# Expert weights in a decoder step: gate and up loads cut into halves of four row blocks

## The chip, the cores and the metric

The kernel runs on one core of a Trainium2 chip, in one launch. The metric is the device time of that core in microseconds (us). One core has a matrix engine (TensorE, PE in the rows, its weight loads PEld), a vector engine (VectorE, DVE), a scalar engine (ScalarE, ACT), GpSimd (POOL) and SyncE (SP), which here issues nearly all of the DMA transfers. The engines run their own instruction streams and meet only at semaphores. Transfers run on 16 DMA engines that all queues share.

## The reference

One step of a two-layer decoder trunk for 256 prompt tokens and 64 sample tokens (320 in all), `D_MODEL` 1024. Layer 0 mixes with mLSTM heads and a short gated convolution, layer 1 with differential attention. Both then do memory attention and a mixture of experts. The change is in the mixture of experts, of which each layer has 32, with 256 hidden columns each, and all of whose weights are read:

```python
y = jnp.zeros_like(x)
for g in range(N_GROUPS):                       # 4 groups of 8 experts
    h = jax.nn.silu(jnp.einsum('nd,edf->nef', x, w_gate[g])) * jnp.einsum('nd,edf->nef', x, w_up[g])
    y = y + jnp.einsum('nef,efd->nd', h * gate[:, g, :, None].astype(h.dtype), w_down[g])
```

Each token uses two experts (top one group, top two in it). Gate, up and down weights are float32: 1 MB for each of the three matrices of an expert, 96 MB for a layer.

## The kernel before

The stages run one after the other: mLSTM, memory attention, experts of layer 0 (`moe`), then attention, memory attention, experts of layer 1, and the final norm. Only the two expert stages matter here.

**Work of an expert stage.** The tokens are gathered into slots by expert, and the experts are taken in `NPAIR` = 16 pairs. In the path that these inputs take, `rounds` is 1 and there is one step q for a pair. TensorE's order is written out by hand in `moe_pe`. A step has `up(q)` (L2369: for each of the 8 row blocks k, and each expert j of the pair, a matmul against gate and up columns, 512 wide), `weigh(q)` (L2382), `select(q)` (L2391), `combine` of an earlier step (L2413), `down` in two halves (L2444) and `transpose_h` (L2453). Up to q = 12 (`TURN`) the order is `up(q)`, `weigh(q)`, `select(q)`, `combine(q-2)`, `down(q-1)`; at 12 a `combine` and a second `down` follow, so that from q = 13 each step does its own `down(q)`.

**Buffers.** `gu` holds two pairs of gate and up weights (slot g % 2, 4 MB each, g counting pairs over both layers). `dws` holds two pairs of down weights (2 MB each), one in `arena` and one in `stg`.

**Loads.** SyncE issues them in program order, and a wait holds all that stand behind it. `load_up(l, p)` waits on `gu_used` until the pair two before has been used. For a step q > 0 that semaphore is raised in `weigh(q)`, after all of `up(q)`. Then it issues four transfers of 1 MB (L469). Only for the last pair of a layer it issues eight of 512 KB, whose second half raises `gu_tail`. `load_down(l, p)` (L478) waits on `dw_used`, which VectorE raises when it has taken the results of the down product two before, and issues two of 1 MB. The order is up(0), up(1), down(0), down(1), up(2), then up(p+1), down(p) for p from 2 to 11, and down(p), up(p+1) for p from 12. Behind the last of layer 0 stand four transfers of attention weights (L446). On TensorE the matmuls at k = 0 wait for `gu_in` of the slot:

```python
if q % rounds == 0 and k == 0:
    pe.wait_ge(gu_in[g % 2], 64 * (g // 2 + 1))
if q % rounds == 0 and k == 4 and p == NPAIR - 1:
    pe.wait_ge(gu_tail, 64 * (l + 1))
```

A row block is one of 8 successive rows that a partition holds (`(p k) f -> p k f`). So a partition's share of one matrix is 8 KB in a row, and half of it 4 KB in a row.

Of the kernel before, what the change touches and what calls it, by code (L numbers as in the profile page):

```python
# [27 lines left out]
NPAIR = NE // 2  # L28
# [104 lines left out]
def build(nc, a, o):  # L133
# [13 lines left out]
    def sem(name):  # L147
        return ctx.enter_context(nc.semaphore(name))
# [119 lines left out]
    def state(h):  # L268
# [76 lines left out]

    names = """const_in tab_in vec_in small_in x_in gate_in cst_ready vec_ps vec_ev tr_ps tr_ev w_hi w_lo w_used
        w_ev in_hi in_lo sq_ready sum_ready std_ready xn_ready gate_ps gneg_ready gln_ready rows_ready
# [4 lines left out]
        gsel_ready rexp_ready gate_ready rank_ps off_ready rc_in moe_done out_mem out_c out_direct ml_ps  # L352
        ml_ev cleared xt_ps xt_hi xt_lo pt_ev pk_ready gate_lo xg_ps xg_act xg_dve z_ps
        zs_act zs_dve zt_ps row_pad qd_ready kt_act kt_dve bs_ps bo_ps bo_ev qp_ready padded id_in mem_hi hsum_ev""".split()
    S = {n: sem(n) for n in names}
# [4 lines left out]
    gu_in = [sem("gu_in0"), sem("gu_in1")]  # L360
    gu_tail = sem("gu_tail")
    dw_in = [sem("dw_in0"), sem("dw_in1")]
# [74 lines left out]
    def _(sp):  # L437
# [73 lines left out]
        for name, n in STREAM:  # L511
# [398 lines left out]
    def mlstm_pool(pool, link):  # L910
# [8 lines left out]
        nc.gpsimd.memset(dmat[rows, :, 384:448], 0.0)  # L919
        nc.gpsimd.memset(wlast[rows, :, 0:8], 0.0).then_inc(S["row_pad"], 1)  # L920
        pool.wait_ge(S["rows_ready"], 1)
# [15 lines left out]
        pool.wait_ge(S["ei_ready"], HA)  # L937
        pool.wait_ge(S["row_pad"], 1)
        decay(0)
        pool.wait_ge(S["w_ev"], sum(UNIT["in_b"]))  # L940
        pool.wait_ge(S["decay_ready"], 1)
        nc.gpsimd.memset(vw[rows], 0.0).then_inc(S["row_pad"], 1)
        pool.wait_ge(S["row_pad"], 2)
        pool.wait_ge(S["ml_ev"], 1)
# [27 lines left out]
    def mlstm_pe(pe):  # L972
# [86 lines left out]
        def numerators(h):  # L1059

            filled = 2 * h - 1
            pe.wait_ge(S["ct_ev"], h + 1)
            if h:
                pe.wait_ge(S["h_ready"], h)
            else:
                pe.wait_ge(S["q_ready"], 1)
                pe.wait_ge(S["s_ready"], HA)
                pe.wait_ge(S["row_pad"], 1)
            for bank, left in ((6, None), (7, ones)):
                first = True  # L1070
                for (tile, n, c, w) in DGROUPS:
                    t0 = T - 64 if tile == 2 else 128 * tile
                    lhs = vtok[:, tile, 128 * h:128 * h + 128] if left is None else ones[:]
                    nc.tensor.matmul(ps[:, bank, t0:t0 + w], lhs, dmat[:, h, c:c + w], start=first, stop=False,
                                     skip_group_check=True)
                    first = False
                if left is None:
                    for b in range(NB):
                        last = nc.tensor.matmul(ps[:, bank, NP + NI * b:NP + NI * b + NI], c0T[:, b, :],
                                                qi[:, h, NI * b:NI * b + NI], start=False, stop=(b == NB - 1),  # L1080
                                                skip_group_check=True)
                        if h:
                            fill(filled, 1, (b,))
                else:
                    last = nc.tensor.matmul(ps[:, bank, NP:T], ones[:], qn[:, h], start=False, stop=True,
                                            skip_group_check=True)
            last.then_inc(S["num_ps"], 1)

        def updates(h):
            pe.wait_ge(S["vw_ready"], h + 1)  # L1090
            if h == 0:
                pe.wait_ge(S["w_ev"], UK)
                pe.wait_ge(S["row_pad"], 2)
            fill_ready(2 * h)
# [852 lines left out]
    def qkv_act(act):  # L1947
        for i in range(12):
            act.wait_ge(S["w_used"], QKV + i + 1)
            if i == 2:  # L1950
                act.wait_ge(S["padded"], 1)
            for g in TURNS.get(i, ()):
# [13 lines left out]
        act.wait_ge(S["padded"], 3)  # L1966
        act.wait_ge(S["rot_done"], 12)
# [29 lines left out]
    def qkv_dve(dve, link):  # L1997
# [51 lines left out]
        dve.wait_ge(S["rot_done"], 16)  # L2049
        dve.wait_ge(S["padded"], 3)  # L2050
        for m in range(2):
# [128 lines left out]
    def route_dve(dve, link, l):  # L2180
# [78 lines left out]
        def slots(c):  # L2259
            for i in range(3):  # L2260
# [19 lines left out]
        V.tensor_tensor(xnh[64:128, 2, KD, 0:NE], gate[64:128, 2], xnh[64:128, 2, KD, 0:NE], ALU.subtract  # L2280
                        ).then_inc(S["gate_lo"], 1)
        for r in range(1, ROUNDS):
# [7 lines left out]
    def moe_pe(pe, l, rounds):  # L2290
        M = ML[l]
        last_step = NPAIR * rounds - 1
        def gather_first():
            pe.wait_ge(S["cleared"], 3 * l + 3)
            pe.wait_ge(S["pk_ready"], 3 * l + 1)
            pe.wait_ge(S["xt_hi"], 6 * l + 6)
# [30 lines left out]
        def gather_next():  # L2327
            pe.wait_ge(S["pk_ready"], 3 * l + 2)
            for k in range(KD + 1):
# [25 lines left out]
        def up(q):  # L2355
# [17 lines left out]

# [482 lines left out]
    def _(pool):  # L2856
# [7 lines left out]
        for name in ("norm_mix_g", "norm_mem_g", "norm_ffn_g"):  # L2864
# [221 lines left out]
```

## Time and profile before

| | |
|---|---|
| median of 3 runs | 1285.54 us (1282.66 to 1286.66) |
| the profiled execution: time, span | 1284.15 us, 1282.8 us |
| TensorE busy | 1204.0 us, 94% of the span |
| VectorE, ScalarE, GpSimd busy | 46%, 31%, 11% |
| DMA: bytes, mean rate, packets | 340.52 MB, 265 GB/s, 114028 |
| mean granted TensorE clock | 0.983 of full speed |

The span is that of one profiled execution on the core; its own time is 1.35 us longer. The expert stage of layer 0 lies between 427 and 668 us of the span, that of layer 1 between 1028 and 1271 us. Times in the rows are counted from the span's start. A 1024.0 KB transfer is 1.049 million bytes, which is how GB/s is counted. "Busy" of a TensorE group counts overlapping matmuls once.

### The profile page before, as it was taken

To read this page: it belongs to the slowest core of one execution; us is meant where nothing else is said; L and a number is where in the kernel's file an instruction comes from. 1 tells how busy PE (TensorE), PEld (TensorE's weight loads), DVE (VectorE), ACT (ScalarE), POOL (GpSimd) and SP (SyncE) were. 2 spreads that over 40 slices of the span, in tenths; PEclk is the share of its full clock that TensorE was granted. 3 is DMA by queue.
4 is the path that set the end of the run, shared out by engine and by line. 5 is a ranking of instruction groups with operands and counts; after the bars stand their busy time and mean duration, and the time that the engine had idled before them with its cause. 6 is when DMAs were issued, how large, how long until landed. Compare 5 with 4: busy or idle time off the path is not lost.

```text
span 1282.8 us, 20881 instructions
## 1 busy us (share of the span) xinstructions
PE 1204.0 (94%) x8548; PEld 738.2 (58%) x8548; DVE 583.9 (46%) x1163; ACT 397.9 (31%) x739; POOL 146.7 (11%) x184
## 2 busy tenths in 40 slices
PE   6999999999998899999999998989999799999996
PEld 5866679877776433333336776767777544333332
DVE  3764368774545522211236667546455541222122
ACT  3533323263443111111125334454444211111113
POOL 5220022111001011000002230001000101001000
PEclk9999999899999899999999999999999899999999
DMA  9575354368659389999974477703775748999994
GB/s 302 155 227 151 102 172 141 115 221 316 228 185 397 134 334 420 420 421 423 419 279 132 135 250 259 256 8 100 296 304 199 321 197 334 416 421 420 421 418 168
DMA packets 114028, 340.52 MB, mean 265 GB/s; under 512 B 7598, under 2 KB 75514, under 8 KB 86272
## 3 DMA queue, kind: packets, MB, share of 16 engines
q1 hardware_dynamic: 108752, 323.51, 67.1%
q0 software_dynamic: 4736, 14.42, 3.6%
q8 instruction: 71, 1.16, 0.4%
q10 hardware_dynamic: 432, 1.11, 0.3%
q14 instruction: 37, 0.30, 0.1%
HBM read 328.48 MB, written 10.54 MB: 264 GB/s over the span
## 4 chain that ended last, share of the span: by engine, by line
PE 76%; DMA 8%; DVE 7%; ACT 5%; issue 2%; POOL 1%; SPq 0%; ACTq 0%; DVEq 0%; POOLq 0%
PE ps L2369 15%; PE ps L614 9%; PE ps L615 8%; PE ps L616 8%; PE ps L2444 6%; DMA arena<-in_w_exp_up 6%; PE ps L2413 4%; PE ps L1530 3%; DVE wl L608 2%; PE ps L1544 2%; PE ps L1569 2%; PE ps L1615 2%; PE ps L1633 2%; DMA stg<-in_w_mem_o 1%; ACT wh L600 1%
## 5 line engine op out<-in xcount | busy, mean ns | idle before, releaser
L2369 PE MATMUL ps<-arena,mkv 128*64 128x512 f32 x1024 | 226.4, 594 | 9.0 <-DMA arena<-in_w_exp_up 8.5
L614 PE MATMUL ps<-bx,wh 128*128 128x320 f16 (+2 forms) x688 | 192.4, 287 | 10.7 <-DVE wl L608 4.1
L615 PE MATMUL ps<-bx,wh 128*128 128x320 f16 (+2 forms) x688 | 192.6, 287 | 0.0
L616 PE MATMUL ps<-bx,wl 128*128 128x320 f16 (+2 forms) x688 | 192.3, 287 | 0.0
L608 DVE SCALAR_TENSOR_TENSOR wl<-stg,wh 128x1024 f16<-128x1024 f32 x122 | 154.6, 1307 | 50.1 <-ACT wh L600 50.1
L600 ACT ACTIVATE wh<-stg 128x1024 f16<-128x1024 f32 x122 | 122.5, 1050 | 146.2 <-PE ps L616 127.8
L2369 PEld LDWEIGHTS ps<-arena,mkv 128*64 128x64 f32 x1024 | 75.6, 137 | 153.9 <-issue 152.2
L2584 DVE TENSOR_TENSOR arena<-ps,arena 128x512 f16<-128x512 f32 x64 | 44.1, 689 | 160.6 <-ACT arena L2530 113.5
L2588 DVE COPY arena<-ps 128x1 f32<-128x1 f32 x32 | 5.1, 159 | 185.3 <-PE ps L2391 185.3
L614 PEld LDWEIGHTS ps<-bx,wh 128*128 128x128 f16 x688 | 68.7, 101 | 34.9 <-issue 14.7
L614 PE MATMUL ps<-arena,wh 128*128 128x320 f16 x288 | 86.6, 301 | 0.9 <-ACT mkv L1212 0.9
L2530 ACT CAST arena<-ps 128x512 f16<-128x512 f32 x64 | 37.5, 585 | 161.1 <-PE ps L2444 161.1
L2635 POOL COPY mkv<-bx 128x576 f32 x60 | 39.9, 668 | 415.1 <-PE ps L2391 301.2
L615 PE MATMUL ps<-arena,wh 128*128 128x320 f16 x288 | 86.5, 300 | 0.0
L616 PE MATMUL ps<-arena,wl 128*128 128x320 f16 x288 | 86.4, 300 | 0.0
L615 PEld LDWEIGHTS ps<-bx,wh 128*128 128x128 f16 x688 | 67.1, 98 | 20.4 <-issue 1.5
L616 PEld LDWEIGHTS ps<-bx,wl 128*128 128x128 f16 x688 | 67.3, 98 | 20.2
L2526 ACT ACTIVATE mkv<-ps 128x256 f32<-128x256 f32 x32 | 12.3, 384 | 214.2 <-PE ps L2369 214.2
L2413 PE MATMUL ps<-arena,rstd 128*128 128x512 f16 x360 | 74.0, 384 | 2.8 <-DVE arena L2584 2.8
L2444 PE MATMUL ps<-stg,mkv 128*64 128x512 f32 x256 | 60.4, 598 | 1.8 <-ACT mkv L2534 1.8
L2444 PE MATMUL ps<-arena,mkv 128*64 128x512 f32 x256 | 60.4, 598 | 0.9 <-ACT mkv L2534 0.9
L1530 PE MATMUL ps<-cst,arena 128*128 128x128 f32 x384 | 52.7, 280 | 3.6 <-ACT arena L1507 2.0
(438 smaller groups left out, 1782.3 us busy)
## 6 DMA issues: line engine op xcount, KB each, us to landing
arena<-in_w_exp_gate SPq DMA_DIRECT2D x60, 1024.0 KB, 12.1
arena<-in_w_exp_up SPq DMA_DIRECT2D x60, 1024.0 KB, 14.2
arena<-in_w_exp_down SPq DMA_DIRECT2D x32, 1024.0 KB, 15.0
stg<-in_w_exp_down SPq DMA_DIRECT2D x32, 1024.0 KB, 16.3
arena<-in_cache_mem_k SPq DMA_DIRECT2D x16, 1024.0 KB, 8.0
arena<-in_cache_mem_v SPq DMA_DIRECT2D x16, 1024.0 KB, 5.0
stg<-in_w_in_a SPq DMA_DIRECT2D x28, 512.0 KB, 4.7
stg<-in_w_qkv_c SPq DMA_DIRECT2D x20, 512.0 KB, 3.6
```

What stands on the lines that cost most here:

```text
L600: nc.scalar.mul(wh[:, s, c], src[:, c], WSCALE).then_inc(S["w_hi"], 1)
L608: nc.vector.scalar_tensor_tensor(wl[:, s, c], src[:, c], WSCALE, wh[:, s, c], ALU.mult, ALU.subtract).then_inc(S["w_lo"], 1)
L614: nc.tensor.matmul(out, wh[:, s, at:at + 128], hi, start=start, stop=False, **flags)
L615: nc.tensor.matmul(out, wh[:, s, at:at + 128], lo, start=False, stop=False, **flags)
L616: return nc.tensor.matmul(out, wl[:, s, at:at + 128], hi, start=False, stop=stop, **flags)
L1530: last = nc.tensor.transpose(ps[:, turn_bank(c, b, f), 256 * i + 128 * t:256 * i + 128 * t + 128], kpg[:, b % 2, t, at:at + 128], ident)
L2369: last = nc.tensor.matmul(ps[64 * j:64 * j + 64, UB, :], xe[:, q % 2, j, k, :], gu[:, g % 2, j, :, k, :], start=(k == 0), stop=(k == KD - ...
L2413: nc.tensor.matmul(out, csel[:, q % 3, 128 * i:128 * i + n], y[:, 512 * half:512 * half + 512], start=(first and y is yh), stop=False, ski ...
L2444: last = nc.tensor.matmul(ps[64 * j:64 * j + 64, (Y0, Y1)[half], :], hT[:, q % 2, 128 * kk + 64 * j:128 * kk + 64 * j + 64], dws[g % 2][:, ...
L2530: nc.scalar.copy(yh[:, 512 * half:512 * half + 512], ps[:, (Y0, Y1)[half], :]).then_inc(M["y_hi"], 1)
L2584: V.tensor_tensor(yl[:, f], ps[:, (Y0, Y1)[half], :], yh[:, f], ALU.subtract).then_inc(M["y_lo"], 1)
L2635: nc.gpsimd.tensor_copy(xe[:, q % 2, j], xg[:, :, ds(at, CAP)]).then_inc(M["xe_ready"], 1)
```

## The change

`load_up` now does for every pair what it did for the last of a layer: it issues row blocks 0 to 3 of both matrices of both experts (four transfers of 512 KB), and then row blocks 4 to 7. The second half raises a semaphore of its own for each slot, `gu_hi`, and TensorE waits for it at k = 4 of each pair. Also each half has its own condition for being loaded. The first waits on a new semaphore `gu_half`, which TensorE raises at k = 3 of `up(q)`, when the slot's first four row blocks have been read; the second waits on `gu_used` as before. To have semaphores for that, some others are merged: `tab_in` into `small_in`, `gate_lo` into `pk_ready`, `row_pad` into `padded`, with the counts that are waited for adapted.

```diff
-    gu_tail = sem("gu_tail")
+    gu_hi = [sem("gu_hi0"), sem("gu_hi1")]
+    gu_half = sem("gu_half")
...
         def load_up(l, p):
             g = NPAIR * l + p
-            if g >= 2:
-                sp.wait_ge(gu_used, g - 1)
-            parts = ((slice(0, 4), gu_in[g % 2]), (slice(4, 8), gu_tail)) if p == NPAIR - 1 else \
-                ((slice(0, 8), gu_in[g % 2]),)
-            for k, arrived in parts:
+            for k, arrived, used in ((slice(0, 4), gu_in[g % 2], gu_half), (slice(4, 8), gu_hi[g % 2], gu_used)):
+                if g >= 2:
+                    sp.wait_ge(used, g - 1)
                 for j in range(2):
                     for m, src in enumerate((w_gate_f, w_up_f)):
                         sp.dma_start(gu[:, g % 2, j, m, k], src[2 * g + j][:, k]).then_inc(arrived, 16)
...
             if name == "qkv":
                 sp.wait_ge(gu_used, NPAIR)
-                sp.wait_ge(S["tab_in"], 16)
+                sp.wait_ge(S["small_in"], SMALL)
...
-            pe.wait_ge(S["gate_lo"], l + 1)
+            pe.wait_ge(S["pk_ready"], 4 * l + 3)
...
-                if q % rounds == 0 and k == 4 and p == NPAIR - 1:
-                    pe.wait_ge(gu_tail, 64 * (l + 1))
+                if q % rounds == 0 and k == 4:
+                    pe.wait_ge(gu_hi[g % 2], 64 * (g // 2 + 1))
                 for j in range(2):
                     last = nc.tensor.matmul(ps[64 * j:64 * j + 64, UB, :], xe[:, q % 2, j, k, :],
                                             gu[:, g % 2, j, :, k, :], start=(k == 0), stop=(k == KD - 1),
                                             skip_group_check=True)
+                if k == 3 and q % rounds == rounds - 1:
+                    last.then_inc(gu_half, 1)
             last.then_inc(M["up_ps"], 1)
```

## Rows read from the trace of the kernel before

**Rows 1.** The page: DMA in 40 equal slices (tenths), and TensorE's wait for weights.

```profile
DMA  9575354368659389999974477703775748999994
...
L2369 PE MATMUL ps<-arena,mkv 128*64 128x512 f32 x1024 | 226.4, 594 | 9.0 <-DMA arena<-in_w_exp_up 8.5
```

**Rows 2.** Timeline of TensorE: start us, us, `up(q)`, [idle before, and its releaser].

```profile
462.01 7.04 PE L2369 MATMUL ps<-arena,mkv 128*64 128x512 f32 x32
...
529.57 7.04 PE L2369 MATMUL ps<-arena,mkv 128*64 128x512 f32 x32
543.08 7.04 PE L2369 MATMUL ps<-arena,mkv 128*64 128x512 f32 x32
...
602.57 7.09 PE L2369 MATMUL ps<-arena,mkv 128*64 128x512 f32 x32 [1.18 <-DMA arena<-in_w_exp_up]
...
651.53 7.04 PE L2369 MATMUL ps<-arena,mkv 128*64 128x512 f32 x32
...
662.09 3.65 PE L2444 MATMUL ps<-stg,mkv 128*64 128x512 f32 x16 [0.46 <-ACT mkv L2534]
...
1207.56 7.09 PE L2369 MATMUL ps<-arena,mkv 128*64 128x512 f32 x32 [1.20 <-DMA arena<-in_w_exp_up]
...
1256.52 7.04 PE L2369 MATMUL ps<-arena,mkv 128*64 128x512 f32 x32
```

**Rows 3.** Chain of waits in order of time: `up(8)` of layer 1, last transfer of `up(12)`.

```profile
1149.20 6.86 PE ps L2369 x32
...
581.25 21.18 DMA arena<-in_w_exp_up
...
1185.68 21.75 DMA arena<-in_w_exp_up
```

**Rows 4.** Timeline of SyncE's queue: start us, us of issuing, transfers.

```profile
462.95 1.39 SPq L478 DMA_DIRECT2D arena<-in_w_exp_down  x2
469.15 0.33 SPq L469 DMA_DIRECT2D arena<-in_w_exp_gate  x1
...
619.34 0.43 SPq L469 DMA_DIRECT2D arena<-in_w_exp_up  x1
...
633.34 2.61 SPq L469 DMA_DIRECT2D arena<-in_w_exp_gate  x1
635.99 2.14 SPq L469 DMA_DIRECT2D arena<-in_w_exp_up  x1
...
1082.40 0.80 SPq L478 DMA_DIRECT2D stg<-in_w_exp_down  x2
1088.60 0.33 SPq L469 DMA_DIRECT2D arena<-in_w_exp_gate  x1
...
1224.33 0.43 SPq L469 DMA_DIRECT2D arena<-in_w_exp_up  x1
...
1240.36 2.13 SPq L469 DMA_DIRECT2D arena<-in_w_exp_up  x1
```

**Rows 5.** Transfers issued at 619.34 (and 1224.33), 635.99, 1240.36 us: KB, us to landing.

```profile
arena<-in_w_exp_up SPq DMA_DIRECT2D x1, 1024.0 KB, 17.9
...
arena<-in_w_exp_up SPq DMA_DIRECT2D x1, 512.0 KB, 16.4
...
arena<-in_w_exp_up SPq DMA_DIRECT2D x1, 512.0 KB, 17.1
```

**Rows 6.** Stretches: engines' busy us, PEclk, DMA share, GB/s.

```profile
593.00:608.00 15.00, 13.82 (x71) 5.22 (x69) 2.90 (x7) 1.83 (x4) 1.33 (x2) 1.00 1.01 420
640.50:650.50 10.00, 9.54 (x52) 3.53 (x50) 1.52 (x4) 1.22 (x3) 0.00 (x0) 1.00 1.02 406
1230.70:1240.70 10.00, 9.54 (x52) 3.39 (x50) 1.52 (x4) 0.76 (x2) 1.33 (x2) 1.00 1.01 422
1245.70:1255.70 10.00, 9.54 (x52) 3.43 (x50) 1.59 (x5) 1.34 (x3) 0.00 (x0) 1.00 1.03 412
655.50:660.00 4.50, 4.50 (x28) 1.68 (x25) 1.04 (x3) 0.38 (x1) 0.00 (x0) 1.00 1.07 353
```

More of the change, by code:

```diff
@@ L343, in build @@
     lt = sq[0:96, 5, :]
-    names = """const_in tab_in vec_in small_in x_in gate_in cst_ready vec_ps vec_ev tr_ps tr_ev w_hi w_lo w_used
+    SMALL = 16 * 5
+    names = """const_in vec_in small_in x_in gate_in cst_ready vec_ps vec_ev tr_ps tr_ev w_hi w_lo w_used
         w_ev in_hi in_lo sq_ready sum_ready std_ready xn_ready gate_ps gneg_ready gln_ready rows_ready
@@ L352, in build @@
         gsel_ready rexp_ready gate_ready rank_ps off_ready rc_in moe_done out_mem out_c out_direct ml_ps
-        ml_ev cleared xt_ps xt_hi xt_lo pt_ev pk_ready gate_lo xg_ps xg_act xg_dve z_ps
-        zs_act zs_dve zt_ps row_pad qd_ready kt_act kt_dve bs_ps bo_ps bo_ev qp_ready padded id_in mem_hi hsum_ev""".split()
+        ml_ev cleared xt_ps xt_hi xt_lo pt_ev pk_ready xg_ps xg_act xg_dve z_ps
+        zs_act zs_dve zt_ps qd_ready kt_act kt_dve bs_ps bo_ps bo_ev qp_ready padded id_in mem_hi hsum_ev""".split()
     S = {n: sem(n) for n in names}
@@ L919, in mlstm_pool @@
         nc.gpsimd.memset(dmat[rows, :, 384:448], 0.0)
-        nc.gpsimd.memset(wlast[rows, :, 0:8], 0.0).then_inc(S["row_pad"], 1)
+        nc.gpsimd.memset(wlast[rows, :, 0:8], 0.0).then_inc(S["padded"], 1)
         pool.wait_ge(S["rows_ready"], 1)
@@ L937, in mlstm_pool @@
         pool.wait_ge(S["ei_ready"], HA)
-        pool.wait_ge(S["row_pad"], 1)
+        pool.wait_ge(S["padded"], 1)
         decay(0)
@@ L941, in mlstm_pool @@
         pool.wait_ge(S["decay_ready"], 1)
-        nc.gpsimd.memset(vw[rows], 0.0).then_inc(S["row_pad"], 1)
-        pool.wait_ge(S["row_pad"], 2)
+        nc.gpsimd.memset(vw[rows], 0.0).then_inc(S["padded"], 1)
+        pool.wait_ge(S["padded"], 2)
         pool.wait_ge(S["ml_ev"], 1)
@@ L1067, in numerators @@
                 pe.wait_ge(S["s_ready"], HA)
-                pe.wait_ge(S["row_pad"], 1)
+                pe.wait_ge(S["padded"], 1)
             for bank, left in ((6, None), (7, ones)):
@@ L1092, in updates @@
                 pe.wait_ge(S["w_ev"], UK)
-                pe.wait_ge(S["row_pad"], 2)
+                pe.wait_ge(S["padded"], 2)
             fill_ready(2 * h)
@@ L1950, in qkv_act @@
             if i == 2:
-                act.wait_ge(S["padded"], 1)
+                act.wait_ge(S["padded"], 3)
             for g in TURNS.get(i, ()):
@@ L1965, in qkv_act @@
                 nc.scalar.activation(lams[:, 2:4], lams[:, 0:2], ACT.Exp).then_inc(S["gln_ready"], 1)
-        act.wait_ge(S["padded"], 3)
+        act.wait_ge(S["padded"], 5)
         act.wait_ge(S["rot_done"], 12)
@@ L2049, in qkv_dve @@
         dve.wait_ge(S["rot_done"], 16)
-        dve.wait_ge(S["padded"], 3)
+        dve.wait_ge(S["padded"], 5)
         for m in range(2):
@@ L2280, in route_dve @@
         V.tensor_tensor(xnh[64:128, 2, KD, 0:NE], gate[64:128, 2], xnh[64:128, 2, KD, 0:NE], ALU.subtract
-                        ).then_inc(S["gate_lo"], 1)
+                        ).then_inc(S["pk_ready"], 1)
         for r in range(1, ROUNDS):
@@ L2294, in gather_first @@
             pe.wait_ge(S["cleared"], 3 * l + 3)
-            pe.wait_ge(S["pk_ready"], 3 * l + 1)
+            pe.wait_ge(S["pk_ready"], 4 * l + 1)
             pe.wait_ge(S["xt_hi"], 6 * l + 6)
@@ L2327, in gather_next @@
         def gather_next():
-            pe.wait_ge(S["pk_ready"], 3 * l + 2)
+            pe.wait_ge(S["pk_ready"], 4 * l + 2)
             for k in range(KD + 1):
@@ L2337, in gather_rest @@
         def gather_rest(k0, k1):
-            pe.wait_ge(S["pk_ready"], 3 * l + 3)
+            pe.wait_ge(S["pk_ready"], 4 * l + 4)
             for k in range(k0, k1):
@@ L2622, in moe_pool @@
         M = ML[l]
-        pool.wait_ge(S["pk_ready"], 3 * l + (2 if rounds == 1 else 3))
+        pool.wait_ge(S["pk_ready"], 4 * l + (2 if rounds == 1 else 4))
         for q in range(1, NPAIR * rounds):
@@ L2874, in _ @@
                        ).then_inc(S["vec_in"], 16)
-        pool.dma_start(ptab[:], a["page_table"].rearrange("b n -> (b n)").unsqueeze(0)).then_inc(S["tab_in"], 16)
+        pool.dma_start(ptab[:], a["page_table"].rearrange("b n -> (b n)").unsqueeze(0)).then_inc(S["small_in"], 16)
         pool.wait_ge(S["w_hi"], 4)
```

1 line of the change is left out of this document (removed).

## The prediction

> **What bounds the kernel now.** I read first the page's slices and its costliest groups [rows 1]. DMA is at nine tenths in the slices of the two expert stages (16 to 20 and 34 to 38), yet TensorE waits for weights for only 8.5 us of the whole span, in seven steps. So an expert stage stands close to both limits, and the question is which of them ends each step. The timeline of TensorE [rows 2] answers it. A step that waits for nothing takes 543.08 - 529.57 = 13.51 us. Counted from `up(8)` at 543.08, `up(12)` should start at 543.08 + 4 x 13.51 = 597.1; it starts at 602.57, 5.5 us late. In layer 1 it should start at 1149.20 + 54.04 = 1203.2 and starts at 1207.56, 4.3 us late [rows 2, 3]. A step moves 6.29 million bytes, which at 421 GB/s, the mean of 420 and 422 in two stretches of 8 KB rows [rows 6], take 14.94 us. The DMA stream falls behind by 1.4 us in each step, until TensorE stands before an unloaded pair. From `up(13)` on TensorE has more to do between two loads (14.04 us, and 21 at the turn), and `up(13)`, `up(14)`, `up(15)` start without a wait. So the late start of `up(12)` is what each layer's end inherits. At most 5.5 + 4.3 = 9.8 us can be had.
>
> The same views show how close the stream still is behind `up(12)`. The last transfer of pair 14 lands at 619.34 + 17.9 = 637.24 and `up(14)` starts at about 651.53 - 14.04 = 637.5. The last of pair 15 lands at 635.99 + 16.4 = 652.4 in layer 0 and 1240.36 + 17.1 = 1257.5 in layer 1, with `up(15)` begun at 651.53 and 1256.52, already in halves [rows 2, 4, 5].
>
> **The change, part by part.**
>
> *Waiting for half a pair.* TensorE needs the second half 7.04 / 2 = 3.52 us after the start of `up`. Before, the whole had to be there at the start. `up(12)`, whose transfers land at 581.25 + 21.18 = 602.43 [rows 3], could thus end 3.5 us earlier with an unchanged stream. The cover for pair 15 does not grow, since it was already loaded and awaited in halves: its second half is needed at 651.53 + 3.52 = 655.05, and from landing to start go 602.57 - 602.43 = 0.14 us, so its slack is 655.05 - 652.54 = 2.5 us; in layer 1 it is 1260.04 - 1257.60 = 2.4 us. TensorE can come forward by this slack and by no more, unless the stream comes forward too.
>
> *Earlier release of the first half.* This helps only where the stream would stand still. Its last pause in layer 0 is before pair 4. The transfers of down(2) start to be issued at 462.95 and take 4.98 us for 2 MB, so the stream would be free at 467.93 on the same scale, but pair 4 is issued at 469.15: a pause of 1.2 us. The new release comes after half of `up(2)`, at 462.01 + 3.52 = 465.5, before 467.93, so the pause goes. What stands before it (several pauses from 414 to 462) brings nothing, as down(2) waits for VectorE until 462.95 either way. In layer 1 the last pause is before pair 5: 1082.40 + 4.98 = 1087.38 against 1088.60, again 1.2 us, and the new release is at about 1085.1 [rows 2, 4]. So the stream comes forward by 1.2 us in each layer.
>
> *Rows of 4 KB.* The pairs loaded in halves so far show the price. While pair 15 was under way, 406 and 412 GB/s were moved, against 421: 4.194 million bytes take 10.33 and 10.18 us in place of 9.96, so 0.37 and 0.22 us more [rows 6]. By landings, from the end of pair 14 to that of pair 15, less 4.98 for down(14): 652.39 - 637.24 - 4.98 = 10.17, and 1257.46 - 1242.23 - 4.98 = 10.25, so 0.21 and 0.29 more [rows 4, 5]. A third reading is far off in size and agrees: 353 GB/s in a stretch whose rows are mostly of 1 KB [rows 6] makes 2.097 million bytes take 0.96 us longer for 1,792 more packets, 0.54 ns each, and 512 more packets for a pair make 0.27 us. I take 0.27 us per pair, the mean of the five. Pairs that pay it after the last pause and before pair 15's landing, beyond pair 15 itself: 11 (4 to 14) in layer 0, 10 (5 to 14) in layer 1. That is 3.0 and 2.7 us of lateness.
>
> The Trainium skill speaks against this change more strongly: DMA: Bandwidth & Descriptors, in Rules for kernel authors, wants 128 partitions and at least 1 MiB per DMA for full bandwidth, and its section Anatomy of one DMA puts 2.0 us of fixed cost beside bytes / 436e9, fitted for GpSimd's path. As an estimate from that page, four more transfers would cost 8 us a pair if nothing overlapped, and some 170 us over the 21 pairs. This trace does not agree for a full queue: pair 15 in eight transfers took 10.2 us against 9.96.
>
> *Issuing.* Eight issues take 8 x 0.43 = 3.4 us of SyncE in place of 1.7, beside a transfer time of 15 us, so nothing on the path. SyncE is held at 633.34 for 2.61 us and at 635.99 for 2.14 us [rows 4]: about nine transfers are then under way (the rest of pair 14, two of down(14), six of pair 15), and each further issue waits for one to end. With halves nine transfers are as little as 4.5 MB, still 10 us of work, so the stream does not run dry, and what is held behind is held with its buffer already free. Cost nothing; were that cover gone, a held issue would be a pause of up to its 2.6 us.
>
> *Waits and merged semaphores.* `up(15)` in layer 0 already has the wait at k = 4 and takes 7.04 us, as `up(7)` does [rows 2]: nothing. The page table's transfer, the low part of the gates and the padded rows are all long done, or were awaited at the same place in the same order: nothing.
>
> **The sum.** TensorE comes forward in layer 0 by 2.5 (slack of pair 15) + 1.2 (pause) - 3.0 (rows of 4 KB) = 0.7 us, in layer 1 by 2.4 + 1.2 - 2.7 = 0.9 us. The other pairs allow more: for `up(12)` it is 3.5 + 1.2 - 9 x 0.27 = 2.3 and 3.5 + 1.2 - 8 x 0.27 = 2.5 us. The last down weights, behind pair 15 by 5 us, are needed only at 662.09 [rows 2]: about 4.5 us of slack, also more. What follows each expert stage starts from TensorE's end and is not short of DMA, so it keeps the gain. Together 1.6 us: the profiled 1284.15 would be 1282.5, and the median of 1285.54, which stands 1.4 above it, 1283.9. What a measurement of this kernel can tell from no change is about 0.3%, 3.9 us.
>
> **The rivals.**
>
> *The price of 4 KB rows does not hold in the long run* (faster). The readings are from one pair at the end of each layer, beside fetches of instructions. At a price of zero the gain is 3.7 + 3.6 = 7.3 us: 1278.2. Each 0.1 us per pair takes 2.1 us off; faster by over 3.9 us needs a price under 0.165. For it: in layer 1 the measured rate is already 412. Against: no reading is below 0.21.
>
> *The rows of 4 KB cost more when all pairs have them* (slower). Place: the stream from pair 4 or 5 on; price p per pair; the gain is 7.3 - 21 p. It is zero at 0.35 and a loss of 3.9 us at 0.53, a rate of 400 GB/s. At 0.6, with each engine's lateness adding up in a stream without pauses, it is -5.3 us: 1290.8. For it: 406 GB/s in layer 0 is 0.37. Against: four readings of five lie below 0.30.
>
> *The stall is only moved to k = 4* (no change). TensorE starts early on the first half of pairs 9 to 15 and stands before the second, and what it gains at `up(12)` is given back by `up(15)`. That is my forecast carried to a price of 0.35: 1285.5.
>
> *Each transfer has a cost of its own that a full queue doesn't hide* (slower). Were it only the 0.43 us in which one is issued [rows 4], four more would make 1.7 us a pair and 36 us over 21 pairs, so 7.3 - 36 = -29 us: 1314. Against: eight transfers of pair 15 took 10.2 us, all costs in. This is the mechanism of the rule in DMA: Bandwidth & Descriptors of the Trainium skill, Rules for kernel authors, that asks for 1 MiB per DMA.
>
> **How the numbers follow.** My forecast, a change of under 0.3%, 0.64: prices from 0.17 to 0.52; its own range is 1282.4 to 1286.2 for 0.20 to 0.38. Of it 0.10 is for the limit case, the stall only moved. The cheap-row rival 0.24, the dear-row rival 0.11, the fixed cost of a transfer 0.01. So faster is 0.24, same 0.64 and slower 0.12. The range has to reach to a price of zero at 1278.2, and to 0.5 at the other end, 1288.7; leaving out a little on either side, 1278.5 to 1288.5.
>
> **What would show it.** Wait of TensorE for weights at k = 0 down from 8.5 us to near nothing, with waits of 0.3 to 2 us inside `up`, at k = 4, from pair 12 to 15 and largest in the last two; `up(12)` done 2 us earlier in each layer, `up(15)` under 1. Packets up by about 17,000 (30 pairs by 512, and 16 small ones for each of 120 more transfers). A stretch of whole pairs at about 414 GB/s (6.29 million bytes in 15.21 us) in place of 421. SyncE held for 1.2 us at many issues. No pause before pair 4 in layer 0. I am wrong if that stretch stays at 421 (then 7 us faster), falls under 409, or if `up(13)` to `up(15)` have slack that I took for used.

## The result: 0.8% slower

The changed kernel takes 1294.27 us (median of 5 runs, 1292.91 to 1298.09) against 1285.54 (1282.66 to 1286.66) for the one before: a ratio of 1.0076, 95% interval 1.0064 to 1.0088. The profiled execution took 1298.09 us, its span is 1296.8. Forecast were 1283.9 and a range of 1278.5 to 1288.5, so the result lies outside it, on the slow side.

The page of the changed kernel, with the rows that answer to [rows 1], the packets, and the 512 KB transfers (KB each, median us from issue to landing):

```profile
DMA  9575354477758499999974577704785769999995
...
DMA packets 131309, 340.53 MB, mean 263 GB/s; under 512 B 9518, under 2 KB 77434, under 8 KB 118912
...
L2368 PE MATMUL ps<-arena,mkv 128*64 128x512 f32 x1024 | 231.3, 602 | 10.1 <-DMA arena<-in_w_exp_up 9.2
...
arena<-in_w_exp_up SPq DMA_DIRECT2D x128, 512.0 KB, 16.2
```

TensorE's wait for weights did not fall: 9.2 us after 8.5. And its `up` groups are busy for 231.3 us in place of 226.4, with the same 1024 matmuls. Both are seen on the timeline of TensorE of the changed kernel, columns as in [rows 2], in layer 0:

```profile
425.47 7.09 PE L2368 MATMUL ps<-arena,mkv 128*64 128x512 f32 x32 [0.43 <-ACT mkv L2508]
...
442.48 0.70 PE L2454 MATMUL ps<-cst,mkv 128*128 128x128 f32 x2 [2.71 <-DVE mkv L2600]
...
444.98 8.86 PE L2368 MATMUL ps<-arena,mkv 128*64 128x512 f32 x32
...
603.41 3.65 PE L2368 MATMUL ps<-arena,mkv 128*64 128x512 f32 x16
...
608.41 3.65 PE L2368 MATMUL ps<-arena,mkv 128*64 128x512 f32 x16 [1.34 <-DMA arena<-in_w_exp_up]
...
643.75 3.65 PE L2368 MATMUL ps<-arena,mkv 128*64 128x512 f32 x16 [0.25 <-DMA arena<-in_w_exp_up]
...
654.40 3.60 PE L2368 MATMUL ps<-arena,mkv 128*64 128x512 f32 x16
...
658.94 3.65 PE L2368 MATMUL ps<-arena,mkv 128*64 128x512 f32 x16 [0.93 <-DMA arena<-in_w_exp_up]
```

The same places before, `up(0)`, the transpose behind it, and `up(1)`:

```profile
427.28 7.39 PE L2369 MATMUL ps<-arena,mkv 128*64 128x512 f32 x32 [0.25 <-ACT mkv L2507]
...
442.59 0.51 PE L2453 MATMUL ps<-cst,mkv 128*128 128x128 f32 x2 [0.71 <-DVE mkv L2599]
443.97 7.09 PE L2369 MATMUL ps<-arena,mkv 128*64 128x512 f32 x32
```

Three things are to be seen. The waits have moved from k = 0 to k = 4 (a group of 32 matmuls is now two of 16, and the second carries the wait), as forecast. But `up(15)` starts at 654.40, where it was 651.53. And a loss that I had not looked for stands at the very start of the stage: from `up(0)` to `up(1)` go 444.98 - 425.47 = 19.5 us, where it was 443.97 - 427.28 = 16.7, and `up(1)` itself then takes 8.86 us in place of 7.09.

The two spans differ by 1296.8 - 1282.8 = 14.0 us. By places: `up(0)` of layer 0 starts 1.8 earlier; from `up(0)` to `up(1)` go 2.8 more in each layer; from `up(1)` to the end of `up(15)` 3.0 (layer 1: 2.4) more, of which 1.8 and 1.7 are the slow `up(1)`; and 4.6 more between the two expert stages. The last can't be put down to the change. That stretch was 369.3 us before and 373.9 after, but it was 372.0 in the kernel below that has only the merged semaphores and takes no longer than the one before, and 368.8 to 373.6 in the others (but 375.3 in that of 64 partitions). TensorE's mean granted clock over it goes along: 0.98 at 369.3, 0.97 at 372.0 and 373.9, 0.99 at 368.8. The median shows only 8.7 us. What has to be explained is the late and slow `up(1)`, 5.7 + 3.5 = 9.2 us in this execution, the slowest of the five (a second trace below has 5.6), and some 2 us in the rest of the two stages.

### The profile page after: what moved, and what is told of

Its sections match the earlier page's. It is cut to its first block, busy times and chain, and to the rows that moved or that the text cites. A ratio compares the mean times of both kernels' runs of the same rounds, so it can differ in the third digit from the quotient of the medians.

```text
span 1296.8 us, 21003 instructions
## 1 busy us (share of the span) xinstructions
PE 1212.5 (93%) x8548; PEld 737.2 (57%) x8548; DVE 583.7 (45%) x1163; ACT 397.9 (31%) x739; POOL 146.7 (11%) x184
## 2 busy tenths in 40 slices
DMA packets 131309, 340.53 MB, mean 263 GB/s; under 512 B 9518, under 2 KB 77434, under 8 KB 118912
## 4 chain that ended last, share of the span: by engine, by line
PE 69%; SPq 9%; DVE 7%; DMA 6%; ACT 4%; issue 2%; POOL 1%; DVEq 0%; POOLq 0%; ACTq 0%
PE ps L2368 10%; PE ps L614 9%; PE ps L616 9%; PE ps L615 9%; SPq L469 7%; DMA arena<-in_w_exp_up 5%; PE ps L2445 5%; PE ps L2414 3%; PE ps L1529 3%; PE ps L1543 2%; DVE wl L608 2%; PE ps L1568 2%; SPq L478 2%; PE ps L1632 2%; PE ps L1614 2%
## 5 line engine op out<-in xcount | busy, mean ns | idle before, releaser
L2368 PE MATMUL ps<-arena,mkv 128*64 128x512 f32 x1024 | 231.3, 602 | 10.1 <-DMA arena<-in_w_exp_up 9.2
L614 PE MATMUL ps<-bx,wh 128*128 128x320 f16 (+2 forms) x688 | 192.7, 287 | 10.1 <-DVE wl L608 4.1
L2527 ACT ACTIVATE mkv<-ps 128x256 f32<-128x256 f32 x32 | 12.3, 383 | 220.9 <-PE ps L2368 220.9
L2445 PE MATMUL ps<-arena,mkv 128*64 128x512 f32 x256 | 60.4, 598 | 0.9 <-ACT mkv L2535 0.9
## 6 DMA issues: line engine op xcount, KB each, us to landing
arena<-in_w_exp_down SPq DMA_DIRECT2D x32, 1024.0 KB, 16.5
stg<-in_w_exp_down SPq DMA_DIRECT2D x32, 1024.0 KB, 16.9
```

Of the source, the lines that this page charges most:

```text
L614: nc.tensor.matmul(out, wh[:, s, at:at + 128], hi, start=start, stop=False, **flags)
L2445: last = nc.tensor.matmul(ps[64 * j:64 * j + 64, (Y0, Y1)[half], :], hT[:, q % 2, 128 * kk + 64 * j:128 * kk + 64 * j + 64], dws[g % 2][:, ...
```

## Why up(1) starts late

VectorE in the changed kernel, from the last instruction ahead of its expert work to the copy of the first result (columns as for TensorE):

```profile
431.09 0.69 DVE L2262 SCALAR_TENSOR_TENSOR arena<-mkv,arena 128x448 f16<-128x448 f32 x1
...
439.56 1.29 DVE L2572 COPY bx<-ps 128x512 f32<-128x512 f32 x2 [7.78 <-issue]
```

And before:

```profile
432.97 0.68 DVE L2263 SCALAR_TENSOR_TENSOR arena<-mkv,arena 128x448 f16<-128x448 f32 x1
...
437.76 0.69 DVE L2571 COPY bx<-ps 128x512 f32<-128x512 f32 x1 [4.10 <-PE ps L2331]
```

Between them VectorE has to go to the expert part of its program. The branch to it is taken in time, 6.6 us after `up(0)` began in the kernel before and 6.5 in the changed one. These are the two, before first (duration in ns, then first and last start in us):

```profile
L2640 DVEq COMPARE_BRANCH  x1: 72/72/72, 433.9 to 433.9; - x1
```

```profile
L2641 DVEq COMPARE_BRANCH  x1: 72/72/72, 432.0 to 432.0; - x1
```

What comes behind the branch is late. The profile calls VectorE's idle 7.78 us "issue": it waited for nothing that the profile shows. The DMA queues do show something (queue: packets, MB, their time as a share of the 16 engines' time). Before, in 434.5 to 435, 7.6 us after `up(0)` began:

```profile
q14 instruction: 1, 0.01, 6.8%
```

In the changed kernel this queue has no packet from 434.5 to 437.5, and one at 437.7, 12.2 us after `up(0)` began. In 437.5 to 438:

```profile
q1 hardware_dynamic: 47, 0.16, 88.9%
...
q14 instruction: 1, 0.01, 4.0%
```

The page counts this queue's packets on the same 16 DMA engines as those of the weights. It does not name the engine whose instructions they are; that they are VectorE's is read from the times, here and in the table near the end. SyncE's queue gives the issues of the weights, before and then in the changed kernel:

```profile
434.91 0.33 SPq L469 DMA_DIRECT2D arena<-in_w_exp_gate  x1
```

```profile
429.17 0.33 SPq L469 DMA_DIRECT2D arena<-in_w_exp_gate  x1
...
432.80 0.33 SPq L469 DMA_DIRECT2D arena<-in_w_exp_gate  x1
```

Before, pair 2's load was first issued behind `up(0)`, at 434.91, just when the instruction packet came. Now the first half is released inside `up(0)`, at k = 3, and is issued 3.7 us after `up(0)` began, ahead of the packet. The packet, and VectorE's first copy, come late. Before, the second copy ended 13.35 us after `up(0)` began (at 440.63); now the first begins at 14.1. TensorE stands idle for 2.71 us, and its granted clock falls from 1.00 to 0.50, the 1.2 GHz level. The stretch in the changed kernel, columns as in [rows 6], PEclk third from the end:

```profile
441.90:448.60 6.70, 6.12 (x17) 2.18 (x19) 1.11 (x3) 0.81 (x2) 1.12 (x2) 0.50 0.18 69
```

`up(1)`, which begins at 444.98 inside this stretch, takes 1.8 us longer. The theory was that the early transfers hold up the fetch of VectorE's instructions; the experiments had to show whether the early release of pair 2 is the cause, whether rows of 4 KB are needed for it, and where the rest of the loss is.

## The experiments

All were timed in five rounds against the kernel before, whose median was 1284.8, 1284.9 and 1284.5 us in the three series; each ratio has its 95% interval. Diffs are against the changed kernel. How long after the start of `up(0)` the instruction packet came is given for layer 0 and then layer 1.

**The changed kernel again.**

> The changed kernel once more, for a second trace. By what its first trace shows, it is slower than before for three reasons: up(1) begins 19.6 us after up(0) in place of 16.8 and itself takes 8.8 in place of 7.1 us (4.6 us a layer), because VectorE's first instruction in the expert code comes 7.8 us after its last one; the rows of 4 KB; and a stretch between the two expert stages that was 4.6 us longer and that I take for chance. If so, ratio 1.007, the first figure again within 0.3 us, and the third one gone. If the stretch between the stages is longer again, it belongs to the change.

1.0064 (1.0048 to 1.0080), 1293.56 us. From `up(0)` to `up(1)` 18.2 and 19.1 us, the instruction packet at 11.9 and 11.8, and VectorE's copy again late:

```profile
440.40 1.29 DVE L2572 COPY bx<-ps 128x512 f32<-128x512 f32 x2 [7.58 <-PE ps L2330]
```

The loss repeats, though not to the 0.3 us that were expected: late and slow `up(1)` make 5.6 us over both layers here, after 9.2. In layer 0 the granted clock was at 0.50 only from 444.5 to 447.7. And the stretch between the expert stages was not back at 369.3 but took 372.9 us. By what was written ahead of this run it would belong to the change; the kernel with only the merged semaphores, further down, has 372.0 at the time of the kernel before, so its length does not show in the medians.

**Pair 2's first half not early.**

```diff
-            for k, arrived, used in ((slice(0, 4), gu_in[g % 2], gu_half), (slice(4, 8), gu_hi[g % 2], gu_used)):
+            early = gu_used if p == 2 else gu_half
+            for k, arrived, used in ((slice(0, 4), gu_in[g % 2], early), (slice(4, 8), gu_hi[g % 2], gu_used)):
```

> The changed kernel, but pair 2 of each layer (the first reload) has its first half issued on gu_used, as before the change. Theory of late code: the transfers issued 3.7 us earlier are under way just as VectorE goes into its expert code and hold up the fetch of its instructions; without them VectorE's gap is 4 us again, up(1) begins 16.8 us after up(0) at full clock, and 9 us are won back: ratio to before 0.999 to 1.001. Theory of slow rows: the price is in the rate of 4 KB rows, which stay, so the ratio stays at 1.006 to 1.008 and up(1) stays late.

1.0019 (1.0010 to 1.0028), 1287.8 us. One condition for one pair in each layer gives back 0.0045 to 0.0057, 6 to 7 us of the 9 that were expected. From `up(0)` to `up(1)` go 16.8 and 16.5 us, the instruction packet is at 7.6 and 7.3 us, and VectorE's copy waits for TensorE again:

```profile
437.80 0.69 DVE L2573 COPY bx<-ps 128x512 f32<-128x512 f32 x1 [4.28 <-PE ps L2331]
...
605.50 3.65 PE L2369 MATMUL ps<-arena,mkv 128*64 128x512 f32 x16 [1.35 <-DMA arena<-in_w_exp_up]
```

The second row is the stall at k = 4 that stays. What is left of the change is still slower than before, by 2.4 us.

**No half early.**

```diff
-((slice(0, 4), gu_in[g % 2], gu_half), (slice(4, 8), gu_hi[g % 2], gu_used)):
+((slice(0, 4), gu_in[g % 2], gu_used), (slice(4, 8), gu_hi[g % 2], gu_used)):
```

> The changed kernel with both halves of every pair waiting for gu_used: halves and the wait at k = 4, but no earlier release. Late code: as with pair 2 alone held back, within 1 us of it. If the early release of later pairs is worth the 1.2 us a layer of my sum, this is 2 us slower than that kernel. Slow rows: ratio 1.006 or more.

1.0049 (1.0035 to 1.0064), 1291.8 us. `up(0)` to `up(1)` is sound (16.4 and 16.4), and yet it loses 6.3 us. Against the kernel above it lacks the early release of the other pairs, and is 0.0030 slower, 3.9 us or 1.9 a layer. So that release does help; by the intervals of the two ratios, taken as independent, it is worth 0.8 to 3.0 a layer, and my 1.2 lies inside that. By the lengths of the two stages in the two traces it is 2.2 and 1.7. And the rows of 4 KB cost more than I had put.

**Only the merged semaphores and the new increment.** Pair 15 alone in halves, as before.

```diff
+    HALVED = (15,)
+    EARLY = ()
...
-            for k, arrived, used in ((slice(0, 4), gu_in[g % 2], gu_half), (slice(4, 8), gu_hi[g % 2], gu_used)):
+            if p in HALVED:
+                parts = ((slice(0, 4), gu_in[g % 2], gu_half if p in EARLY else gu_used), (slice(4, 8), gu_hi[g % 2], gu_used))
+            else:
+                parts = ((slice(0, 8), gu_in[g % 2], gu_used),)
+            for k, arrived, used in parts:
```

> The changed kernel's merged semaphores and its new gu_half, but transfers and waits of gate and up weights as before (only the last pair in halves). Both theories: ratio 1.000 within 0.1%. A third, that the merged semaphores hold something up: 1.002 or more, with up(1) late.

1.0001 (0.9989 to 1.0013), 1285.21 us. They cost nothing.

**Pair 2 alone.** The same with `HALVED = (2, 15)` and `EARLY = (2,)`.

> Loads as before the change, but pair 2 of each layer is loaded in halves, its first half issued after k = 3 of up(0). Late code: this alone brings the cost at up(1): it begins 19.6 us after up(0) and runs at a lower clock, ratio 1.005 to 1.007. Slow rows: two pairs of 32 in rows of 4 KB cost 0.3 us each, ratio 1.000 to 1.001.

1.0061 (1.0044 to 1.0077), 1292.73 us, 7.5 us more than the kernel above. Pair 2 in halves, with four early transfers in each layer, makes nearly the whole loss. (The halves alone don't: further down they are kept, with one early transfer in place of four.) Its TensorE and VectorE:

```profile
423.50 7.09 PE L2375 MATMUL ps<-arena,mkv 128*64 128x512 f32 x32 [0.25 <-ACT mkv L2515]
...
443.54 7.28 PE L2375 MATMUL ps<-arena,mkv 128*64 128x512 f32 x32
...
438.12 1.29 DVE L2579 COPY bx<-ps 128x512 f32<-128x512 f32 x2 [8.36 <-PE ps L2352]
```

20.0 us to `up(1)` (20.2 in layer 1), the copies 14.6 us after `up(0)` started. The profile names a group of matmuls as releaser, which was long done; the packet of the instruction queue comes at 12.8 and 13.0 us.

**Other weights in the same place.** With the policy of the merged kernel, the 2 MB of pair 1's down weights, in rows of 8 KB, are issued after k = 3 of `up(0)`, in place of pair 2's half.

```diff
+                sp.wait_ge(gu_half, NPAIR * l + 1)
                 for j in range(2):
                     sp.dma_start(dws[g % 2][:, j], w_down_f[2 * g + j]).then_inc(dw_in[g % 2], 16)
```

> Loads of gate and up as before the change (1 MB, rows of 8 KB), but the down weights of pair 1 (2 MB in rows of 8 KB, needed 40 us later) are issued after k = 3 of up(0) and not in the first batch. So other data are under way when VectorE goes into its expert code. Late code: any traffic there delays it; up(1) begins 18 to 20 us after up(0), ratio 1.003 to 1.007. Slow rows, or something peculiar to transfers of 4 KB rows or to the gate and up weights: up(1) begins 16.8 us after up(0), ratio 1.000 to 1.001.

1.0004 (0.9991 to 1.0017), 1285.25 us: no loss, where the theory had 1.003 to 1.007. Yet the fetch is late here too. The packet comes at 10.3 and 10.1 us, some 2.5 later than before, and the copy at 12.2. First the stretch, then the queues in 437.5 to 438, then VectorE:

```profile
434.00:440.00 6.00, 6.00 (x52) 4.23 (x49) 0.23 (x2) 2.12 (x5) 0.00 (x0) 1.00 1.01 422
```

```profile
q1 hardware_dynamic: 27, 0.22, 104.5%
...
q14 instruction: 1, 0.01, 3.9%
```

```profile
439.85 1.36 DVE L2580 COPY bx<-ps 128x512 f32<-128x512 f32 x2 [5.77 <-PE ps L2337]
```

The copies run back to back and end at 441.2, 13.6 us after `up(0)` began, 0.2 later than before, and `up(1)` comes after 16.9 and 16.5 us. So 2.5 us of delay are covered by what VectorE had to spare between and ahead of its two copies, and more than that isn't: these other weights delay the packet as well, but a loss needs more delay than this.

**The same bytes in rows of 4 KB.** As above, with these 2 MB in four transfers of 512 KB.

```diff
-                for j in range(2):
-                    sp.dma_start(dws[g % 2][:, j], w_down_f[2 * g + j]).then_inc(dw_in[g % 2], 16)
+            for k in ((slice(0, 1), slice(1, 2)) if p == 1 else (slice(0, 2),)):
+                for j in range(2):
+                    sp.dma_start(dws[g % 2][:, j, k], w_down_f[2 * g + j][:, k]).then_inc(dw_in[g % 2], 16)
```

> As the kernel that issues the down weights of pair 1 after k = 3 of up(0) (ratio 1.0004; there VectorE's instruction packet came 10.0 us after the start of up(0) in place of 7.5), but those 2 MB go in four transfers with rows of 4 KB. If rows of 4 KB in a just started stream are what holds the packet up to 12 us, it comes there at 11.5 to 13 us here too, the stream starts at 200 to 300 GB/s, up(1) begins 18 to 20 us after up(0), and the ratio is 1.003 to 1.006. If it is something about the gate and up weights, 10 us and 1.000 to 1.001.

1.0025 (1.0013 to 1.0038), 1288.19 us, a smaller loss than the 1.003 to 1.006 expected. The packet comes at 11.5 and 11.1 us, `up(1)` 17.7 and 17.3 us after `up(0)`, 0.8 later than with long rows in each layer. (That is 1.6 of the 2.7 us between the two ratios; the rest isn't located.) Stretch and VectorE:

```profile
434.00:440.00 6.00, 6.00 (x54) 4.53 (x51) 0.00 (x0) 2.13 (x5) 0.00 (x0) 1.00 0.99 322
```

```profile
440.58 1.29 DVE L2582 COPY bx<-ps 128x512 f32<-128x512 f32 x2 [7.10 <-PE ps L2338]
```

The early bytes are the same 2 MB, and in the same six microseconds 322 GB/s are moved in place of 422, with the engines as busy. So the early bytes are under way for longer, the fetch is later again, and now it goes past what is covered. The number of transfers has doubled here along with the shorter rows; the kernel after next tells the two apart.

**Only a quarter of pair 2 early.** `HALVED = (2, 15)`, `EARLY = (2,)`, and of the first half only the first transfer, 512 KB.

```diff
                     for m, src in enumerate((w_gate_f, w_up_f)):
+                        if p == 2 and j == 0 and m == 1:
+                            sp.wait_ge(gu_used, g - 1)
```

> As the kernel with pair 2 alone in halves (ratio 1.0061), but only the first of the four early transfers, 512 KB, is issued after k = 3 of up(0); the other three and the second half wait for gu_used. If the instruction packet waits for the traffic that is queued before it, it comes at 7.5 to 9 us, and the ratio is 1.000 to 1.001. If any early issue is enough, it comes at 12 us and the ratio is 1.005 to 1.007.

1.0010 (0.9999 to 1.0021), 1285.78 us. The packet is at 7.3 and 7.9 us, `up(1)` after 16.7 and 16.9. Pair 2 is in halves here as well, so the loss hangs on the early bytes and not on the halves. With 512 KB the fetch isn't late, with 2 MB it is; how the delay grows between them wasn't tried.

**The count of transfers or the length of rows.** As the kernel with no half early, but one transfer takes a half of both experts: four of 1 MB for a pair, the rows still of 4 KB.

```diff
-                for j in range(2):
-                    for m, src in enumerate((w_gate_f, w_up_f)):
-                        sp.dma_start(gu[:, g % 2, j, m, k], src[2 * g + j][:, k]).then_inc(arrived, 16)
+                for m, src in enumerate((w_gate_e, w_up_e)):
+                    sp.dma_start(gu[:, g % 2, :, m, k], src[:, 2 * g:2 * g + 2, k]).then_inc(arrived, 16)
```

> As the kernel with halves and no early release (ratio 1.0049, 413 GB/s in a full stretch, and 200 to 360 GB/s for the first 7 us after each pause), but a transfer takes the half of both experts, so four transfers of 1 MB with rows of 4 KB make a pair. If the lower rate is a matter of rows of 4 KB, it stays at 413 and the slow starts stay: ratio about 1.005. If it is a matter of the number of transfers, 421 GB/s and no slow starts: ratio 0.997 to 1.001.

1.0067 (1.0043 to 1.0091), 1293.57 us, not faster than with 512 KB (1.0035 to 1.0064). Its stretch of whole pairs, 490 to 540 us, then that of the changed kernel and that of the kernel before:

```profile
490.00:540.00 50.00, 50.00 (x256) 17.89 (x252) 10.22 (x25) 6.04 (x14) 5.33 (x8) 1.00 1.02 412
```

```profile
490.00:540.00 50.00, 50.00 (x254) 17.77 (x253) 10.42 (x26) 7.04 (x16) 3.99 (x6) 1.00 1.02 412
```

```profile
490.00:540.00 50.00, 50.00 (x258) 17.85 (x256) 10.78 (x26) 5.87 (x13) 5.33 (x8) 1.00 1.01 421
```

Transfers of 1 MB and of 512 KB both move 412 GB/s. The start of the stream at pair 4, which comes up below, stays slow too (292 GB/s in 468 to 475 us, 335 in 471 to 478). So it is the rows that cost, and the number of transfers costs nothing that can be seen.

**Long rows in small transfers.** The opposite case: eight transfers a pair, but each of 64 partitions by 8 KB. All eight are awaited at k = 0.

```diff
+                parts = ((slice(0, 64), slice(0, 8), gu_in[g % 2]), (slice(64, 128), slice(0, 8), gu_hi[g % 2]))
...
+                        sp.dma_start(gu[rows, g % 2, j, m, k], src[2 * g + j][rows, k]).then_inc(arrived, 16)
```

> Gate and up weights in eight transfers of 512 KB as in the changed kernel, but each takes 64 partitions with rows of 8 KB, all awaited at k = 0 and released on gu_used. It doubles the number of transfers and leaves the row size. If the lower rate is a matter of row size, a full stretch moves 421 GB/s and the ratio is 1.000 to 1.001. If it is a matter of the number of transfers, the stretch moves 413 GB/s and the stage ends 3 us a layer later: ratio 1.004 to 1.005.

1.2568 (1.2517 to 1.2619), 1619.94 us, and useless for its question: halves by partition bring a cost of their own that drowns the rest.

```profile
490.00:540.00 50.00, 27.41 (x124) 9.74 (x122) 5.80 (x14) 3.66 (x8) 2.67 (x4) 0.81 1.01 238
```

The engines are fully busy (1.01) and move 238 GB/s. The Trainium skill, in DMA: Bandwidth & Descriptors, Rules for kernel authors, advises one transfer to 128 partitions in place of two to disjoint halves. This case agrees that the two are worse, with 238 GB/s against 421. Why they are that much worse no run here shows.

**Halves only where TensorE waits.** `HALVED = (12, 13, 14, 15)`, `EARLY = ()`.

> Halves only for pairs 12 to 15, all on gu_used; the others as before. By my sum: up(12) can start on its half, and pair 15 has 2.5 us of slack less 3 x 0.27 for the rows of 4 KB, so 1.7 us a layer, 3.4 in all: ratio 0.9973. If rows of 4 KB cost more than that, less; 1.000 or more would mean that the slack at pair 15 was not there.

0.9974 (0.9961 to 0.9987), 1281.39 us: faster than both kernels. TensorE in layer 0, `up(11)`, `up(12)`, and the two halves of `up(15)`:

```profile
588.01 7.09 PE L2375 MATMUL ps<-arena,mkv 128*64 128x512 f32 x32 [1.18 <-DMA arena<-in_w_exp_up]
...
601.57 7.04 PE L2375 MATMUL ps<-arena,mkv 128*64 128x512 f32 x32
...
650.49 3.60 PE L2375 MATMUL ps<-arena,mkv 128*64 128x512 f32 x16
654.59 3.65 PE L2375 MATMUL ps<-arena,mkv 128*64 128x512 f32 x16 [0.50 <-DMA arena<-in_w_exp_up]
```

`up(12)` follows 13.56 us after `up(11)` without a wait, and 13.6 in layer 1, where it was 14.9. `up(15)` of layer 0 waits for half a microsecond before its second half: it is now as early as its weights allow. From `up(1)` to the end of `up(15)` go 213.7 and 216.9 us against 214.6 and 218.9 before.

**And with the pause before pair 4 closed.** `HALVED = (4, 5, 12, 13, 14, 15)`, `EARLY = (4, 5)`.

> The fastest kernel so far (pairs 12 to 15 in halves, ratio 0.9974), and pairs 4 and 5 in halves as well, their first half on gu_half, to fill the last pause of the stream in each layer. By my sum 1.2 us a layer less two pairs at 0.32: 0.6 us a layer, ratio 0.9965. If rows of 4 KB move at half the rate for the first 7 us there, some 2 us a layer are lost in place of it: ratio 0.998 to 1.000.

0.9992 (0.9980 to 1.0004), 1283.73 us: of the 3.3 us gained above, 2.3 are lost again (0.0018 between two ratios whose intervals are 0.0012 and 0.0013 either way, which is at the edge of noise), though the stream starts earlier. Its stretch at pair 4's first half; then one of the merged kernel, where pair 4 has long rows and is issued 1.1 us later than in the third kernel; then the same stretch of the kernel with no half early:

```profile
468.00:475.00 7.00, 7.00 (x40) 2.64 (x38) 2.21 (x5) 1.24 (x3) 1.33 (x2) 1.00 0.99 330
```

```profile
471.00:478.00 7.00, 7.00 (x36) 2.41 (x34) 1.38 (x3) 1.45 (x3) 0.00 (x0) 1.00 1.01 426
```

```profile
471.00:478.00 7.00, 7.00 (x36) 2.36 (x34) 1.38 (x3) 1.45 (x3) 0.00 (x0) 1.00 0.97 307
```

The engines are busy in all three (0.97 to 1.01), but the rows of 4 KB move 307 to 330 GB/s there, and not the 412 of the steady stage. 7 us at 307 in place of 426 are 0.83 MB, or 2.0 us of the stream at 421 GB/s; in layer 1 the same kernels show 283 against 422 in 1095 to 1102, 2.3 us. Pair 5 is issued at 1094.09 in the one and at 1090.65 in the other, though, so that window does not compare like with like. The landings bear the size out all the same, as is worked out below. TensorE in this kernel accordingly waits already at `up(8)` in layer 0:

```profile
544.02 7.09 PE L2375 MATMUL ps<-arena,mkv 128*64 128x512 f32 x32 [0.80 <-DMA arena<-in_w_exp_up]
```

## Why the prediction was wrong

**The step that failed** is *Earlier release of the first half*: "What stands before it (several pauses from 414 to 462) brings nothing, as down(2) waits for VectorE until 462.95 either way." It brings no gain, that was right; but I took a pause of the stream for empty time and asked only who would gain if it were filled. It was the time in which VectorE's instructions came over the same engines. A term that I had put at nothing, pair 2's four transfers in that pause, costs 7.5 us over both layers by the kernel that has only this, and 6 to 7 by the one that has all but this. The prediction's own range could not hold that: none of the four rivals was about what other traffic the earlier transfers would meet.

**Rows of 4 KB.** I took 0.27 us a pair, and in a stream long under way that was nearly right: 412 and 413 GB/s in 50 us (forecast: 414) against 421, and where TensorE waits in each step, `up(12)` comes 15.21 us after `up(11)` in place of 14.91, 0.30 a pair. 21 pairs make 6.3 us, where I had 5.7. (The two windows at pair 15 hold no packet of an instruction queue, so those readings were not taken "beside fetches of instructions".) What the price left out is the start of the stream. In the kernel with no half early, the second half of pair 15 is there at 656.78 and 1267.71 us, 189.1 after the first issue of pair 4 (467.70) and 173.6 after that of pair 5 (1094.09); before it was 183.3 and 168.9. The stream is late by 5.8 + 4.7 = 10.5 us, and 10.5 - 6.3 = 4.2 belong to no price per pair. The slow stretches of 7 us are of that size (2.0 and, by the unlike window, 2.3). Less 4.9 for the slack of pair 15, the stages should be 5.6 us longer; in the trace they are 3.3 + 2.3 = 5.6, and by the ratio the kernel loses 6.3.

**The pause before pair 4 (5).** I took 1.2 us a layer; the early release of all pairs but 2 is worth 1.9 (0.8 to 3.0). The kernel without pair 2's stands at 6.3 - 3.9 = 2.4 us by that, but the 3.9 is the difference of these two kernels, so it is no separate proof.

**Waiting for half a pair** was right, size and place. My bound of 2.5 and 2.4 us by pair 15's slack, less 0.30 for each of the three pairs 12 to 14 that newly pay, gives 1.6 + 1.5, together about 3.1 us for the kernel with halves at the tail alone; it gained 3.3 against the kernel before by the ratio, 1285.21 - 1281.39 = 3.8 against the merged kernel by the medians, and 0.9 + 2.1 = 3.0 in its trace. The Trainium skill, in Perfetto Trace Analysis, DMA Optimizations, says that splitting a transfer may let work start sooner; here this holds for the four pairs for which TensorE waits, and is paid for in the twelve others.

**Issuing, merged semaphores, number of transfers**: costed at nothing, and nothing they are. SyncE is held as forecast; its queue in the changed kernel:

```profile
526.05 1.08 SPq L469 DMA_DIRECT2D arena<-in_w_exp_gate  x1
527.17 1.08 SPq L469 DMA_DIRECT2D arena<-in_w_exp_up  x1
```

1.08 us each, forecast 1.2, and no harm. (By their issues and landings ten transfers were under way at 635.99 us before, not nine.) Packets rose by 131,309 - 114,028 = 17,281, forecast 17,000.

**The rivals.** *Moved to k = 4*: the profile looks like it (waits of 1.38 us in `up(10)` and 1.34 in `up(12)`, 0.25 in `up(14)`, 0.93 in `up(15)`, where I had expected the largest in the last two), and the 2.4 us that are left without pair 2's early half are near it, but it doesn't make the 8.7 us. *Dear rows*: nearer to the truth than my forecast; at the steady price alone the kernel would have been 7.3 - 6.3 = 1.0 us faster still. So even the part of the loss that is left without pair 2 took the slow stretch at pair 4 (5) as well.

**What stays open**: why rows of 4 KB move at 300 GB/s with busy engines early in the stage and at 412 later. The stretch is slow behind a pause and, in the kernel with pairs 4 and 5 early, with no pause ahead of it. And that the fetch of VectorE's instructions is what makes the copies late is inferred from times. They fit closely, in us after the start of `up(0)`, layer 0 and layer 1:

| kernel | early bytes | last instruction packet ahead of the copy | first copy starts | between |
|---|---|---|---|---|
| before | none | 7.6, 7.8 | 10.5, 10.6 | copy waits for TensorE |
| pair 2 not early | none | 7.6, 7.3 | 10.6, 10.2 | copy waits for TensorE |
| a quarter early | 512 KB, rows of 4 KB | 7.3, 7.9 | 10.4, 10.7 | copy waits for TensorE |
| down weights | 2 MB, rows of 8 KB | 10.3, 10.1 | 12.2, 12.0 | 1.9, 1.8 |
| down weights | 2 MB, rows of 4 KB | 11.5, 11.1 | 13.3, 13.0 | 1.8, 1.9 |
| changed, again | 2 MB, rows of 4 KB | 11.9, 11.8 | 13.7, 13.6 | 1.8, 1.8 |
| changed | 2 MB, rows of 4 KB | 12.2, 12.3 | 14.1, 14.2 | 1.8, 1.9 |
| pair 2 alone | 2 MB, rows of 4 KB | 12.8, 13.0 | 14.6, 14.8 | 1.8, 1.8 |

Where the packet is late, the copy starts 1.8 to 1.9 us behind it, in all ten cases, while the packet itself moves by 2.9 us. Where it comes at 7.9 or sooner, it would let the copy go by 9.8, and the copy starts at 10.2 to 10.7 with TensorE's result. (Not every packet of this queue is VectorE's: in the kernel of 64 partitions one comes at 9.2 us in layer 1, and the copy is in time at 10.2.) What isn't shown is when each packet was asked for, and so whether it stood behind the weights in a queue or was asked for late. No kernel moved the fetch itself, for instance by having VectorE enter its expert code earlier.

## What to carry to other kernels

Before a transfer is moved forward into a pause of the DMA stream, look at what else uses the engines in that pause: here VectorE went on to another part of its program just then, the packets of its instructions ran over them, and with its slack of 2.5 us the pause was not free. A split of transfers pays where the consumer waits for them and costs everywhere else, so split the few that are waited for: here four pairs of sixteen gained 0.26%, and all sixteen with the early release lost 0.76%. A price that is read at one place of a stream holds for that place; read it at the start of the stream too.

## What was not expected of the hardware

- A packet on the queue of instructions came 6.7 to 7.9 us after `up(0)` began with the engines nearly idle or 512 KB under way, at 10.1 to 10.3 with 2 MB in rows of 8 KB, and at 11.1 to 13.0 with 2 MB in rows of 4 KB. VectorE's branch was taken at 6.5 to 6.6 before and in the changed kernel, and its next instruction started 1.8 to 1.9 us behind the late packet. In the profile the engine's idle time is put down to "issue" or to an engine long done.
- Rows of 4 KB by 128 partitions move 412 to 413 GB/s in a long stream, against 421 for 8 KB, in transfers of 512 KB and of 1 MB alike; in some stretches of 6 to 7 us, at pair 2 and at pair 4 or 5, 282 to 342 GB/s with the engines busy for 0.93 to 0.99.
- 64 partitions by 8 KB move 238 GB/s with the engines fully busy.
- In an idle time of TensorE of 2.7 us its granted clock fell to 0.50 and stayed there for 6.7 us, and an `up` of 7.09 us took 8.86. In layer 0 of two other executions with a late `up(1)` it was at 0.50 for 3.2 us, and `up(1)` took 7.3 and 8.5.
